# The last stage of a decoder step: two large products by a seven-product scheme instead of eight

## The reference, cut to what matters

```
m = g_r * ((o_r * silu(zg_r)) @ proj_r) + g_n * ((o_n * silu(zg_n)) @ proj_n)
h = h + m @ w_out                       # (tokens x 1024) @ (1024 x 1024)
e = rmsnorm(p @ w_pe, pe_norm_g)        # (tokens x 256) @ (256 x 1024)
h = h + sigmoid(h @ w_pg) * e           # (tokens x 1024) @ (1024 x 1024)
y = rmsnorm(h, final_norm_g)
```

## Time and profile before

| | us |
|---|---|
| median of 3 runs (lowest, highest) | 1885.51 (1884.55, 1889.64) |
| the profiled execution, its own time | 1887.97 |
| its span, first to last instruction | 1886.0 |
| PE busy in the span | 1760.9 (93%) |
| DVE, ACT, POOL busy | 683.9, 550.5, 375.5 |
| `finish_tokens`: first PE instruction to the end of the span | 1600.84 to 1886.0 |

### The profile page before, as it was taken

The page is one execution under the profiler, slowest core; times in us unless marked ns, Lnnn a source line. Parts: engine busy times, 40 slices in busy tenths (PEclk is TensorE's granted clock), DMA queues, the critical chain, the costliest instruction groups (busy, mean ns, idle before and its releaser), DMA issues. The chain is left out here.

```text
span 1886.0 us, 40234 instructions
## 1 busy us (share of the span) xinstructions
PE 1760.9 (93%) x17784; PEld 1156.0 (61%) x17784; DVE 683.9 (36%) x1448; ACT 550.5 (29%) x1141; POOL 375.5 (20%) x438
## 2 busy tenths in 40 slices
PE   7999899999999898889988599899999999999997
PEld 5666566666666555666666589766566666444443
DVE  3101345555554171466665664351200001112122
ACT  4111334343432101466664011223300000222223
POOL 0111222222221000344443321123101001010101
PEclk9999899999999999799999799899999999999999
DMA  4111000010010350630000995458522110401010
GB/s 150 45 37 47 2 14 14 14 25 14 14 25 14 95 94 0 156 126 2 1 2 1 313 294 224 153 130 190 119 72 72 36 45 1 179 23 45 23 45 23
DMA packets 116066, 135.83 MB, mean 72 GB/s; under 512 B 48220, under 2 KB 97061, under 8 KB 111326
## 3 DMA queue, kind: packets, MB, share of 16 engines
q1 hardware_dynamic: 106576, 83.95, 16.3%
q0 software_dynamic: 9216, 49.29, 8.5%
q10 hardware_dynamic: 102, 0.03, 0.0%
HBM read 120.64 MB, written 16.62 MB: 73 GB/s over the span
## 5 line engine op out<-in xcount | busy, mean ns | idle before, releaser
L725 PE MATMUL ps<-xnT,rw_side_w 128*128 128x344 f32 x576 | 205.5, 481 | 0.0
L443 PE MATMUL ps<-xnT,w_z 128*128 128x344 f32 x624 | 184.1, 456 | 2.3 <-DVE xnT L537 1.3
L443 PEld LDWEIGHTS ps<-xnT,w_z 128*128 128x128 f32 x624 | 119.0, 192 | 64.0 <-issue 3.3
L1928 POOL TENSOR_SCALAR probs<-probs,row_sums,gates 128x63 f32<-128x63 f32 (+6 forms) x148 | 95.2, 662 | 259.7 <-DVE row_sums L1888 259.7
L725 PEld LDWEIGHTS ps<-xnT,rw_side_w 128*128 128x128 f32 x576 | 99.8, 192 | 40.7 <-issue 4.1
L2180 PE MATMUL ps<-xnT,zT 128*128 128x344 f32 x384 | 120.7, 463 | 0.0
L2665 PE MATMUL ps<-xnT,ring_k 128*128 128x344 f32 x384 | 116.7, 458 | 2.2 <-PEq L81 2.2
L2669 PE MATMUL ps<-zT,ring_k 128*128 128x344 f32 x384 | 115.0, 452 | 0.0
L2849 PE MATMUL ps<-w_pg,h_T 128*128 128x512 f32 x256 | 111.3, 592 | 1.0 <-ACT h_T L2878 1.0
L2793 PE MATMUL ps<-w_out,mT 128*128 128x512 f32 x256 | 111.6, 593 | 0.5 <-DVE h_sample L2933 0.5
L2665 PEld LDWEIGHTS ps<-xnT,ring_k 128*128 128x128 f32 x384 | 73.8, 192 | 41.3 <-issue 4.0
(11 more groups left out here) (510 smaller groups left out, 2810.7 us busy)
## 6 DMA issues: line engine op xcount, KB each, us to landing
w_z<-in_w_in_dram SPq DMA_DIRECT2D x13, 512.0 KB, 3.8
xnT_kept<-xnT SPq DMA_DIRECT2D x1, 4128.0 KB, 13.5
xnT<-xnT_kept SPq DMA_DIRECT2D x1, 4128.0 KB, 13.4
x_tok<-in_x_prompt_dram SPq DMA_DIRECT2D x8, 512.0 KB, 7.6
rw_side_w<-in_w_in_dram SPq DMA_DIRECT2D x16, 256.0 KB, 3.3
zT<-in_w_in_dram SPq DMA_DIRECT2D x8, 512.0 KB, 5.7
ring_k<-in_w_in_dram SPq DMA_DIRECT2D x8, 512.0 KB, 4.0
w_out<-in_w_out_dram SPq DMA_DIRECT2D x1, 4096.0 KB
```

What stands on the lines that cost most here:

```text
L443: last = nc.tensor.matmul(k.ps[:, u % 6, 0:CG], w[:, n % w_ring, c, :], k.xnT[:, c, g * CG:(g + 1) * CG], start=(c == 0), stop=(c == KC - 1))
L725: ins = nc.tensor.matmul(k.ps[:, SIDE_BANKS[g % 2], 0:CG], w.side[:, t % 2, c, :], k.xnT[:, c, g % 3 * CG:(g % 3 + 1) * CG], start=(c == 0 ...
L1928: nc.gpsimd.tensor_scalar(every, every, ls[:, at:at + 1], k.gates[:, i, gate:gate + 1], ALU.mult, ALU.mult).then_inc(scaled, 1)
```

## The change

In `merge_branches` the two small work tiles move into a free part of `zT`, and DVE additionally makes three sums of quarters of `w_out` (each 128 x 2048 elements), behind groups 15, 17 and 19 of its 24. In `finish_tokens` the token tiles are taken in four pairs (tile p with tile p + 4), and each of the two large products is done as a 2 x 2 block product by the scheme of Strassen and Winograd: seven products of 4 chunks x 512 columns (`PRODUCTS`) for a pair instead of eight. Sums of the token side (`operand_sums`, four per pair and product) and the remaining sums of the weights are made by DVE. All pairs' `w_out` products come first, then all `w_pg` products. The turned `h` is copied into `mT` in place of the `m` that was there, `h` is kept for all eight tiles, and `w_out`'s room is used for the gates and for `e` once it is free. Three of the seven results are first copied out of PSUM by ACT in the `w_pg` half.

```diff
+                if u == 15:
+                    dve.wait_ge(in_wo, 16)
+                    nc.vector.tensor_tensor(k.wt[:, 0], k.w_out[:, lo, right], k.w_out[:, lo, left], ALU.subtract).then_inc(made, 1)
...
+PRODUCTS = ("P1", "P5", "P6", "P2", "P7", "P3", "P4")
...
+            return {"P1": (part(0, 0, p), w[:, 0:4, cols(0)], a, True),
+                    "P5": (sums[:, s, 0], wot[:, 0], BCC, True),
+                    "P6": (sums[:, s, 1], wot[:, 1], a, False),
+                    "P2": (part(0, 1, p), w[:, 4:8, cols(0)], BB, True),
+                    "P7": (sums[:, s, 2], w[:, 0:4, cols(1)], a, False),
+                    "P3": (sums[:, s, 3], w[:, 4:8, cols(1)], BCC, False),
+                    "P4": (part(1, 1, p), wot[:, 2], a, False)}[name]
...
+            load_x(2)
+            load_x(3)
             sp.dma_start(we[:], x.w_pe[0].rearrange("(c p) n -> p c n", p=P)).then_inc(in_g, 16)
...
+            load_x(7)
+            sp.dma_start(wg[:], x.w_pg[0].rearrange("(c p) n -> p c n", p=P)).then_inc(in_wg, 16)
...
+            def product(name, u):
+                left, right, bank, first = factors(name, u)
+                for c in range(4):
+                    last = nc.tensor.matmul(k.ps[:, bank, :], left[:, c, :], right[:, c, :], start=(first and c == 0),
+                                            stop=(c == 3), skip_group_check=True)
+                return last
...
+                elif name == "P6":
+                    pe.wait_ge(s_made, 4 * u + 2)
+                    pe.wait_ge(tg_made, 2)
+                    pe.wait_ge(g_copy, 3 * p + 1)
+                elif name == "P7":
+                    pe.wait_ge(s_made, 4 * u + 3)
+                    pe.wait_ge(tg_made, 3)
+                    pe.wait_ge(g_copy, 3 * p + 3)
...
+            sample_out()
+            for name in PRODUCTS:
+                out_product(name, 0)
+                if name == "P2":
+                    small_turns()
+            sample_embed()
+            pe.wait_ge(sht_out, 1)
+            for name in PRODUCTS:
+                out_product(name, 1)
+                if name == "P1":
+                    e_total()
+            sample_gate()
+            for name in PRODUCTS:
+                out_product(name, 2)
+                if name == "P6":
+                    y_total()
+                elif name == "P3":
+                    turn(0)
+            for name in PRODUCTS:
+                out_product(name, 3)
+                if name == "P1":
+                    turn(1)
+                elif name == "P2":
+                    turn(2)
+            for p in range(NPR):
+                for name in PRODUCTS:
+                    gate_product(name, p)
+                    if name == "P1" and p == 0:
+                        turn(3)
+                    elif name == "P2":
+                        embed(2 * p)
+                    elif name == "P7":
+                        embed(2 * p + 1)
...
+            def norms(p):
+                square_y(2 * p, 0, True, y0_p, 2 * p + 1)
+                square_y(2 * p, 1, False, y0_p, 2 * p + 2)
+                root_y(2 * p)
+                square_y(2 * p + 1, 1, True, y0_v, 2 * p + 1)
+                square_y(2 * p + 1, 0, False, y0_v, 2 * p + 2)
+                root_y(2 * p + 1)
...
+            for p in range(NPR):
+                if p:
+                    norms(p - 1)
+                copy_out(p, 0, 1, 0, 0, BA[p % 2])
+                if p == 0:
+                    turned(6)
+                    turned(7)
+                copy_out(p, 1, 2, 1, 1, BCC)
+                copy_out(p, 2, 3, 0, 1, BA[p % 2])
+                square_e(2 * p)
+                square_e(2 * p + 1)
+                sigmoid(p, 0, 0, 1)
+                sigmoid(p, 1, 1, 2)
+                sigmoid(p, 0, 1, 3)
+                sigmoid(p, 1, 0, 0)
+            norms(NPR - 1)
...
+            for p in range(NPR):
+                for n in range(2):
+                    a = et[:, p % 2, 0, cols(n)]
+                    pool.wait_ge(e_t, 4 * p + n + 1)
+                    pool.wait_ge(sig, 4 * p + (1, 3)[n])
+                    nc.gpsimd.tensor_tensor(a, a, sg[:, p % 2, 0, cols(n)], ALU.mult).then_inc(gm_p, 1)
+                    pool.wait_ge(gm_p, 2 * p + n + 1)
+                    nc.gpsimd.tensor_tensor(h[:, 2 * p, cols(n)], a, h[:, 2 * p, cols(n)], ALU.add).then_inc(y0_p, 1)
...
+                nc.vector.tensor_tensor(to[0], part(1, 0, p), part(1, 1, p), ALU.add).then_inc(s_made, 1)
+                nc.vector.tensor_tensor(to[2], part(0, 0, p), part(1, 0, p), ALU.subtract)
...
+            def residual(p, group, j, half, bank, first):
+                dve.wait_ge(h_ps, 7 * p + group)
...
+                a = h[:, 2 * p + j, cols(half)]
+                nc.vector.tensor_tensor(a, k.ps[:, bank, :], a, ALU.add).then_inc(h_out, 1)
...
+            sums_of_gate_weights(2)
+            sums_of_gate_weights(3)
+            for p in range(NPR):
+                if p:
+                    gated(p - 1, 0, 1)
+                    normed(2 * p - 2)
+                    normed(2 * p - 1)
+                if p + 1 < NPR:
+                    operand_sums(NPR + p + 1)
+                add_out(p, 4, 0, 0, BB)
+                scaled_e(2 * p)
+                add_out(p, 5, 1, 1, BA[p % 2])
+                scaled_e(2 * p + 1)
+                add_out(p, 6, 0, 1, BCC)
+                gated(p, 1, 0)
+            gated(NPR - 1, 0, 1)
+            normed(NT - 2)
+            normed(NT - 1)
```

More of the change, by code:

```diff
@@ L2719, in finish_tokens @@
[L2719 removed]
+        in_wg = ctx.sem("in_wg")
+        in_x = [ctx.sem(f"in_xr{n}") for n in range(NT)]
         in_g, in_xs, in_p = ctx.sem("in_g"), ctx.sem("in_xs"), ctx.sem("in_p")
[L2721 to L2723 removed]
@@ new lines, in turn @@
+            def turn(p):
+                pe.wait_ge(h_out, 7 * (p + 1))
+                if p == 0:
+                    pe.wait_ge(sgat, 1)
+                    pe.wait_ge(sy_root, 1)
+                else:
+                    pe.wait_ge(ht_out, 2 * p)
+                for j in range(2):
+                    for c in range(KC):
+                        last = nc.tensor.transpose(k.ps[:, 4 + 2 * j + c // 4, (c % 4) * P:(c % 4 + 1) * P],
+                                                   h[:, 2 * p + j, c * P:(c + 1) * P], k.ident[:])
+                    last.then_inc(ht_ps, 1)
@@ new lines, in sample_embed, with sample_gate @@
+            def sample_embed():
+                pe.wait_ge(p_o, 5)
+                pe.wait_ge(in_g, 48)
+                for c in range(2):
+                    for t in range(4):
+                        rows, at = quarter(t)
+                        last = nc.tensor.matmul(k.ps[rows, 4, 0:Q], pT[:, c, LO:TT], we[:, c, at], start=(c == 0), stop=(c == 1))
+                last.then_inc(se_ps, 1)
+            def sample_gate():
+                pe.wait_ge(sht_out, 1)
+                pe.wait_ge(in_wg, 16)
+                for c in range(KC):
+                    for t in range(4):
+                        rows, at = quarter(t)
+                        last = nc.tensor.matmul(k.ps[rows, 5, 0:Q], hsT[:, c % 2, 32 * (c // 2):32 * (c // 2 + 1)], wg[:, c, at],
+                                                start=(c == 0), stop=(c == KC - 1))
+                last.then_inc(sg_ps, 1)
@@ L2781, in _ @@
[L2781 to L2826, removed]
@@ L2853, in _, with turned, copy_out @@
         @block.scalar
         def _(act):
+            def turned(v):
+                act.wait_ge(ht_ps, v + 1)
+                at = 4 + 2 * (v % 2)
+                nc.scalar.activation(k.mT[:, :, tile_rows(v)], k.ps[:, at:at + 2, :].rearrange("p b (c n) -> p (b c) n", n=P),
+                                     ACT.Copy).then_inc(ht_out, 1)
+            def copy_out(p, n, group, j, half, bank):
+                act.wait_ge(g_ps, 7 * p + group)
+                if p >= 2:
+                    act.wait_ge(y_sq, 4 * (p - 1))
+                nc.scalar.activation(sg[:, p % 2, j, cols(half)], k.ps[:, bank, :], ACT.Copy).then_inc(g_copy, 1)
@@ new lines, in _ @@
+            for v in range(2 * (NPR - 1)):
+                turned(v)
+            for p in range(NPR):
+                if p:
+                    norms(p - 1)
+                copy_out(p, 0, 1, 0, 0, BA[p % 2])
+                if p == 0:
+                    turned(6)
[8 more added lines that the diff above has]
+                sigmoid(p, 1, 0, 0)
@@ new lines, in residual, with add_out @@
+            def residual(p, group, j, half, bank, first):
+                dve.wait_ge(h_ps, 7 * p + group)
+                if first:
+                    dve.wait_ge(in_x[2 * p + j], 16)
+                else:
+                    dve.wait_ge(h_out, 7 * p + group - 1)
+                a = h[:, 2 * p + j, cols(half)]
+                nc.vector.tensor_tensor(a, k.ps[:, bank, :], a, ALU.add).then_inc(h_out, 1)
+            def add_out(p, group, j, half, bank):
+                dve.wait_ge(g_ps, 7 * p + group)
```

(3 more changed lines are left out.)

441 lines of the change are left out of this document (277 added, 164 removed).

## The result

| | before | after |
|---|---|---|
| median (lowest to highest) of 4 runs each, us | 1885.03 (1883.9 to 1889.64) | 1856.72 (1853.92 to 1858.67) |
| ratio after / before, 95% interval | | 0.9844 (0.9822 to 0.9867) |
| span of the profiled execution | 1886.0 | 1853.0 |
| first PE instruction of the last stage to the end of the span | 285.2 | 255.7 |
| PE's part of it / tail behind PE | 275.1 / 10.0 | 243.5 / 12.3 |

The median is 28.3 us shorter; 25.4 were forecast (1860.1). The last stage itself is 29.5 us shorter. The profiled span is 33.0 us shorter, but 3.6 of these lie ahead of the last stage, which starts at 1597.28 instead of 1600.84, in code that the change doesn't touch: the stage before, `merge_branches`, starts at 1370.0 instead of 1373.6 already.

What follows compares the result with a forecast made beforehand. The prediction took PE to bound the last stage: 27.5 + 4.4 + 1.7 = 33.6 us saved, less 5.4 of waits and 2.8 of tail, gives 25.4, so 1885.5 - 25.4 = 1860.1 us; range 1851 to 1867.

Steps and rivals of the forecast that it cites:

- The bound: Last stage: PE is busy throughout at full clock, so a removed PE instruction saves its whole pace, 0.4294 us.
- part 1: Both large products: 224 PE instructions instead of 256 each, 64 fewer at 0.4294 us, saving 27.5 us.
- Part 2: PE's gaps in the last stage: five idle times go, 4.4 us, and the sample product with `w_pg` saves 1.7.
- Part 3: Added DVE sums, bank handovers and `x` loads moved ahead, in `merge_branches` and the last stage: hidden, costed at nothing.
- Part 4: `w_pg` half: P6 waits for ACT's copy of P1, 1.8 us at three of four pairs, 5.4 us lost.
- Part 5: Chain behind PE's last product: now runs for two tiles, tail 12.8 us against 10.0, 2.8 longer.
- The sum: Whole run: PE ends at 1847.8 and the span at 1860.6, 25.4 us less than 1886.0.
- A: Rival, `w_pg` half: the waits of P6 don't occur; gain 32.2 us, time 1853.3; chance 0.17.
- B: Rival, `w_pg` half: granted clock falls for some us; time 1865, up to 1869 with DVE behind; chance 0.14.
- C: Rival, handovers of PE's four banks: all 56 products wait, 0.54 us each, 30.2 us; time 1890; chance 0.04.
- D: Rival, large products: PE does not keep pace 0.4294; 2% more costs 3.8 us, time 1864; chance 0.05.

Runs made afterwards that it cites:

- e5: Changed kernel plus an eighth product that nothing reads, in each pair of both large products; 1883.99 us, 0.999 of the kernel before.
- e8: Changed kernel with the sample products with `w_pe` and `w_pg` back in the first pair, behind the small transpositions; 1864.06 us, 0.987 of the kernel before.
- e7: Changed kernel with P5 and P1 swapped in the `w_out` half, so P6 follows P1 without a product between; 1861.45 us, 0.986 of the kernel before.
- e2: Changed kernel with ACT's copy of P1 moved ahead of the norms of the pair before; 1856.65 us, 0.981 of the kernel before.
- e6: Changed kernel with DVE's two gating sums for tile p+4 cut to 1 column from 512, waits kept; 1850.26 us, 0.980 of the kernel before.
- e3: Changed kernel with POOL's gated sums made by DVE, POOL without work in the `w_pg` half; 1854.87 us, 0.979 of the kernel before.
- e10: Changed kernel with a dummy Sqrt in front of `norms`, so ACT loads the table while waiting for POOL; 1854.88 us, 0.982 of the kernel before.
- e4: Changed kernel with the edits of e2 and e3, plus reordered squares and an early table load in the last pair; 1853.58 us, 0.980 of the kernel before.
- e9: Changed kernel with DVE making all gating sums, and the last pair reordered so tile 6 is done first; 1852.28 us, 0.980 of the kernel before.

## Why the prediction was right, step by step

- **The time**: 1856.72 lies 3.4 us under the forecast of 1860.1, just outside the forecast's own band (1857 to 1863) and well inside the range. The mechanism came as said; sizes and one piece of luck, the first group's clock, make the difference.
- **The bound and part 1** hold: pace 0.429, and e5 prices 64 instructions at 27.4 us (forecast 27.5).
- **Part 2**: the five gaps are gone, and `sample_gate` takes 3.66 us (forecast 3.43). e8 shows the other way round what that place costs: its own idle times and a product at a lower clock add 7.2 us. One statement was wrong: the first sample product does not "stay as it is". It took 1.5 us less here, because the clock came back sooner, and in other traces of the same changed kernel 5.35 and 6.53 us. So it is luck and no part of the change, and 1.5 of the 4.1 us by which the stage beat the forecast.
- **Part 3**: the added work costs nothing: `merge_branches` keeps its 227.24 us in the two traces, and there is no idle time in the `w_out` half. That a handover is hidden by the product in between is shown by e7, for P6. That 1.5 MB of loads moved ahead don't matter where the products now stand is seen in the trace only. e8 shows that the landing of `w_pg` would matter earlier, and that it came 2.4 us later, not 3.9.
- **Part 4**: the mechanism, its place and its number of times are right. That ACT's order makes the wait is shown by e2, that the turns of DVE and POOL do by e6; e3 and e10 fit, since any edit that takes over a microsecond out of the chain ends a wait of 1.0. Its size was off: 1.0 us of idle time, 1.2 lost with PE's start, in place of 1.8; 3.5 in all, not 5.4. Two terms were mis-sized. POOL's last sum ended at 3.2, not 3.45: the four began 0.3 us later than reckoned but took 6.3 us, not 6.9, so that each of three turns cost 0.4 us and not 0.6. And ACT needed 4.7 us from there to the copy's end, not 5.2, because its instructions start some 0.1 us before the one ahead ends.
- **Part 5**: tail 12.3 (forecast 12.8). By the same two terms DVE's last result came 8.9 us behind PE's end, not 9.7. A third term took back 0.25: from there to the end it was 3.4 us, not the 3.1 of before. The tile ahead is now stored 1.2 us in front of the last two halves, and e4, where it is 0.85, took 3.7; that the stores hold each other up fits this, but no run tried it apart.
- **The sum**: 285.2 - 25.4 = 259.8 was forecast for the stage, 255.7 came: 1.9 from the waits, 1.5 from the first group, 0.5 from the tail; `sample_gate` took back 0.2, and 0.4 stay unexplained.
- **The rivals**: A (no waits) fell: the waits are there, three times 1.0 us, and e2, e3, e6 and e10 each take them away. Their real price, 3.5 us, lies between A's nothing and the 5.4 forecast. B fell: no clock below 1.00 from the first product to PE's end; a wait of 1.0 us three times left it whole. C is priced above. D fell: 0.429.

## What to carry to other kernels

Where one engine is busy to the last tenth, as PE is here, a scheme that removes an eighth of its products can give their whole time back, if each result that another engine must take away has one product as cover. Price that cover: without it a handover cost 0.8 to 0.9 us of idle time here. Sums of two SBUF operands on DVE and on POOL at the same time alternated here, one whole instruction after the other, so work "spread" over both may finish later than on DVE alone. And a table load belongs where its engine waits anyway. What the seven-product scheme costs in rounding is not measured here.

## What the runs showed of the hardware that was not expected

- A pair has eight gating sums. On DVE alone (e3) all eight took 5.4 us, from 1851.11 to 1856.50 in the last pair. With four of them on POOL and four on DVE, 6.9 us passed from the first to the last (1773.14 to 1780.00), 0.5 of it DVE's wait for a sigmoid: the two engines together were slower than one.
- A sum of one column on DVE, 0.16 us alone, took 1.23 when it started just behind a sum of POOL (e6).
- After the barrier in front of the last stage (3.2 us of idle PE) the same 64 instructions took 4.93 to 6.60 us in the traces. In the slowest PEclk is 0.50 over the stage's first 4.5 us, in the fastest 0.71.
- In four traces (e2, e3, e4, e9) an earlier stage, which waits for indirect gathers, took 10 us more than in the others (147.5 instead of 137 us), in code that is the same. PE waits there 7.3 to 7.5 us for a copy of DVE (line 2122) that is on time in the others. In each of the four kernels the traced execution is the longest of all its runs (e9: 1867.63, the others 1848.91 to 1853.42). What causes it stays open.
